# Seven-product output projections of 12 of 22 hidden chunks, inside the chain of the input projections

## The reference, cut to what matters

```python
def swiglu(x, w_in, w_out):
    gate, up = jnp.split(x @ w_in, 2, axis=-1)
    return (jax.nn.silu(gate) * up) @ w_out
# x = x + 1/2 * swiglu(rms_norm(x)); D_MODEL = 1024, D_FF = 2816
```

## Time and profile before

| | us |
|---|---|
| median of 3 runs | 2073.2 (2071.76 to 2074.09) |
| profiled execution | 2073.98 |
| span of its trace | 2071.8 |
| TensorE busy | 2041.6 (99%) |
| VectorE busy | 1329.3 (64%) |
| GpSimd busy | 1297.1 (63%) |
| ScalarE busy | 867.2 (42%) |

### The profile page before, as it was taken

The page is one execution under the profiler, slowest core; times in us unless marked ns, Lnnn a source line. Parts: engine busy times, 40 slices in busy tenths (PEclk is TensorE's granted clock), DMA queues, the critical chain, the costliest instruction groups (busy, mean ns, idle before and its releaser), DMA issues.

```text
span 2071.8 us, 41329 instructions
## 1 busy us (share of the span) xinstructions
PE 2041.6 (99%) x16420; PEld 1994.5 (96%) x16420; DVE 1329.3 (64%) x1873; ACT 867.2 (42%) x1651; POOL 1297.1 (63%) x999
## 2 busy tenths in 40 slices
PE   9999999999999999999999999999999999999998
PEld 8999999999989999999999999999998799999997
DVE  7861884425756882497578439844876678816853
ACT  6641662121574661364256226511432446505631
POOL 6775777654425676677767757765643267766773
PEclk9999999999999999999999999999999999999999
DMA  4321333122112232223123322333210232322231
GB/s 158 102 105 69 103 110 122 65 103 71 68 43 92 82 111 92 76 101 125 69 82 103 112 66 99 117 112 112 88 62 31 90 102 82 118 77 101 93 123 45
DMA packets 31702, 190.61 MB, mean 92 GB/s; under 512 B 3888, under 2 KB 6448, under 8 KB 13104
## 3 DMA queue, kind: packets, MB, share of 16 engines
q1 hardware_dynamic: 24192, 173.43, 24.3%
q10 hardware_dynamic: 7344, 14.89, 2.0%
HBM read 180.81 MB, written 7.50 MB: 91 GB/s over the span
## 4 chain that ended last, share of the span: by engine, by line
PE 52%; DVE 20%; POOL 10%; ACT 8%; issue 6%; DMA 2%; ACTq 0%; DVEq 0%; POOLq 0%; SPq 0%
PE ps L615 36%; PE ps L630 8%; DVE tg L2362 5%; POOL sil L526 4%; DVE tg L2359 4%; POOL ws L507 3%; DMA wraw<-in_wf_in 2%; POOL wl L573 2%; DVE a L2271 2%; DVE s L2300 2%; ACT sil L1761 2%; DVE ps L2280 2%; ACT ps L1692 1%; ACT ws L1725 1%; DVE ps L2338 1%
## 5 line engine op out<-in xcount | busy, mean ns | idle before, releaser
L690 PE MATMUL ps<-tt,ws 128*128 128x272 f32 x3840 | 526.2, 290 | 7.2 <-DVE ws L2304 6.4
L690 PEld LDWEIGHTS ps<-tt,ws 128*128 128x128 f32 x3840 | 500.0, 189 | 10.7 <-DVE ws L2304 7.3
L615 PE MATMUL ps<-a,wh 128*128 128x272 f32 x3028 | 500.3, 287 | 1.6 <-POOL wl L573 1.6
L573 POOL TENSOR_TENSOR wl<-wraw,wh 128x512 fp32r<-128x512 f32 (+1 forms) x351 | 475.2, 1376 | 12.7
L569 POOL TENSOR_SCALAR wh<-wraw 128x1024 fp32r<-128x1024 f32 (+2 forms) x152 | 167.7, 1103 | 471.2 <-PE ps L615 244.7
L615 PEld LDWEIGHTS ps<-a,wh 128*128 128x128 f32 x3028 | 423.6, 188 | 3.7 <-POOL wl L573 3.4
L690 PE MATMUL ps<-u,ws 128*128 128x272 f32 x2880 | 401.6, 288 | 1.1 <-DVE tg L2350 0.6
L507 POOL TENSOR_TENSOR ws<-wraw,ws 128x512 fp32r<-128x512 f32 x240 | 330.9, 1391 | 99.1 <-ACT ws L1700 55.6
L690 PEld LDWEIGHTS ps<-u,ws 128*128 128x128 f32 x2880 | 376.6, 188 | 2.4 <-issue 1.6
L615 PE MATMUL ps<-a,wl 128*128 128x272 f32 x1514 | 311.9, 287 | 0.0
L507 POOL TENSOR_TENSOR ws<-s,ws 128x512 fp32r<-128x512 f32 x160 | 209.0, 1306 | 142.3 <-ACT ws L1725 142.3
(11 more groups left out here) (391 smaller groups left out, 2929.4 us busy)
## 6 DMA issues: line engine op xcount, KB each, us to landing
wraw<-in_wf_in SPq DMA_DIRECT2D x87, 1024.0 KB, 4.8
wraw<-in_wf_out SPq DMA_DIRECT2D x32, 1408.0 KB, 6.0
wraw<-in_w_ab SPq DMA_DIRECT2D x12, 1024.0 KB, 4.8
wraw<-in_w_cd SPq DMA_DIRECT2D x10, 1024.0 KB, 4.9
wraw<-in_w_abo SPq DMA_DIRECT2D x8, 512.0 KB, 3.6
wraw<-in_w_cdo SPq DMA_DIRECT2D x8, 512.0 KB, 3.6
wraw<-in_w_bv SPq DMA_DIRECT2D x2, 1024.0 KB, 4.9
out_y<-yout ACTq DMA_DIRECT2D x14, 136.0 KB, 1.9
```

What stands on the lines that cost most here:

```text
L573: piece = nc.gpsimd.tensor_tensor(wl[:, s, some], wraw[:, par_, s * K * P + some.start: s * K * P + some.stop], wh[:, s, some].bitcast(F32 ...
L615: last = nc.tensor.matmul(bank(b0 + 2 * s + half, 0, HT), w[:, s, k * P:(k + 1) * P], act_t[:, k0 + k, part, half * HT:(half + 1) * HT], s ...
L690: last = nc.tensor.matmul(bank(b, 0, HT), ws[weights][w][:, i * P:(i + 1) * P], moving[:, part], start=(start and i == 0 and w == 0 and pa ...
```

## The change

The 22 hidden chunks are now three groups of 6, 6 and 10. The output projections of the first two groups take seven products too. They are 4 periods each of K = 6, of kind "out", put into the same chain, which now runs without a break: input periods of chunks 2 to 6, four output periods of chunks 0 to 5, input periods of chunks 7 to 12, four output periods of chunks 6 to 11, and input periods of chunks 13 to 21. The last group stays plain with K = 10.

An output period needs sums of the activation blocks of each pair of chunks (2k, 2k+1). When the odd chunk's `glu` is done, GpSimd makes four sums of 272 columns (`h_sums`), ScalarE their high parts (`e_highs`, `t3_high`), VectorE their low parts (`h_lows`, `t3_low`). This happens in one iteration of the chain per pair, six per block f; below it is called a *sum iteration*. Only half of an even chunk is still split by `glu_high` and `glu_low`. The result of an output period is added into x by VectorE (`first_row`, `second_row`). Layout of the tiles and numbering of semaphores follow. Blank lines are dropped from the diff:

```diff
-G = 2
-GK = FC // G
+GROUPS = [6, 6, 10]
-SEVENS = FC - LEAD
+SEVENS = 20 + 8
...
+        a = place("a", [11, 2, T], F32R, a_at)
+        th_at = a_at + 7 * 8 * T
+        th = place("th", [3, 3, 2, HT], F32R, th_at)
+        at[0] = th_at + 72 * HT
-        te = [place(f"te{e}", [2, HT], F32, a_at + 8 * T * 9 + 8 * HT * e) for e in range(TILES7)]
+        te = [place(f"te{e}", [2, HT], F32, th_at + 8 * HT * e) for e in range(TILES7)]
...
         SEQ = []
         for f in range(4):
-            chains = []
-            for g in range(G):
-                first = STAGE[FFN_STAGE[f] + 2 * g][1] - g * GK
-                lo, hi = max(g * GK, LEAD), (g + 1) * GK
-                chains.append([Period(first + i, SEVENS * f + i - LEAD, i, DC, (hi - 1 - i) % 2, i == hi - 1)
-                             for i in range(lo, hi)])
-            SEQ.append(chains)
+            first = STAGE[FFN_STAGE[f]][1] + LEAD
+            todo = ([("in", 0, i) for i in range(LEAD, 7)] + [("out", 0, i) for i in range(4)] +
+                    [("in", 1, i) for i in range(7, 13)] + [("out", 1, i) for i in range(4)] +
+                    [("in", 2, i) for i in range(13, FC)])
+            SEQ.append([Period(first + j, SEVENS * f + j, kind, i, DC if kind == "in" else GROUPS[g], g,
+                               (SEVENS - 1 - j) % 2, j == SEVENS - 1) for j, (kind, g, i) in enumerate(todo)])
...
+        def chunk_before(last):
+            return last.i if last and last.kind == "in" else None if last else LEAD - 1
+        def ripe(last):
+            i = chunk_before(last)
+            return i // 2 if i is not None and i < 12 and i % 2 else None
         def quarter(p, part):
...
+            def h_sums(f, k):
+                t = unit(f, TILES7 + k)
+                pool.wait_ge(glu_done, FC * f + 2 * k + 2)
+                h11, h12, h21, h22 = tg[:, 1, 0:HT], tg[:, 1, HT:T], tg[:, 2, 0:HT], tg[:, 2, HT:T]
+                e = he[slot(2 * k + 2)]
+                nc.gpsimd.tensor_tensor(e[:, T3, :], h22, h12, ALU.subtract).then_inc(t_sum, 1)
+                nc.gpsimd.tensor_tensor(e[:, 1, :], h11, h12, ALU.subtract).then_inc(t_sum, 1)
+                pool.wait_ge(t_sum, 4 * t + 1)
+                nc.gpsimd.tensor_tensor(e[:, 0, :], e[:, T3, :], h11, ALU.add).then_inc(t_sum, 1)
+                pool.wait_ge(t_sum, 4 * t + 3)
+                nc.gpsimd.tensor_tensor(e[:, 2, :], e[:, 0, :], h21, ALU.subtract).then_inc(t_sum, 1)
...
+                low_t(f, 3)
+                due = None
                 for n, p in enumerate(seq):
-                    period(seq[n - 1] if n else None, p, seq[n + 1] if n + 1 < len(seq) else None)
+                    if due is not None:
+                        h_sums(f, due)
+                    last = seq[n - 1] if n else None
+                    period(last, p, seq[n + 1] if n + 1 < len(seq) else None)
+                    due = ripe(last)
             for n, (arr, count, K) in enumerate(stages):
                 first, c0, c1, _, _ = STAGE[n]
...
+                    product(0, c0 + i, K, act_t, ready, base, slots=slots)
+                    product(1, c1 + i, K, act_t, ready, base, slots=slots)
                     if body:
                         body(i - lo)
-            def sevens(f, g):
-                seq = SEQ[f][g]
-                def operand(what, i):
+            def sevens(f):
+                seq = SEQ[f]
+                def operand(p, what, i):
+                    if p.kind == "in":
...
+                    if p.kind == "in":
+                        return tt[:, i, what]
+                    if what == T3:
+                        return rows[:, lo, :, HT:T]
+                    return th[:, i, {E2: 0, E1: 1, T4: 2}[what]]
                 def made(p, what, i):
...
-                nc.scalar.copy(a[:, slot(i), 0, :], tg[:, 1 + i % 2, :]).then_inc(act_high, 1)
-            def seven_acts(f, g, before, between):
-                seq = SEQ[f][g]
+                if i >= 2 and i % 2 == 0 and i <= 12:
+                    act.wait_ge(e_low, unit(f, TILES7 + i // 2 - 1) + 1)
+                    act.wait_ge(t3_ready, unit(f, TILES7 + i // 2 - 1) + 1)
+                cols_ = slice(0, HT if i < 12 and i % 2 == 0 else T)
+                nc.scalar.copy(a[:, slot(i), 0, cols_], tg[:, 1 + i % 2, cols_]).then_inc(act_high, 1)
+            def e_highs(f, k):
+                e = he[slot(2 * k + 2)]
+                act.wait_ge(t_sum, 4 * unit(f, TILES7 + k) + 4)
+                nc.scalar.activation(th[:, k % 3, 0, 0, :], e[:, 0, :], ACT.Identity, scale=-1.0)
+                nc.scalar.copy(th[:, k % 3, 1:3, 0, :], e[:, 1:3, :]).then_inc(e_high, 1)
+            def t3_high(f, k):
+                nc.scalar.copy(a[:, slot(2 * k), 0, HT:T], he[slot(2 * k + 2)][:, T3, :]).then_inc(t_high, 1)
...
                         high_a11(next_, p)
                     high_a22(p)
-                    if last:
+                    if last and last.kind == "in":
                         gate(last)
+                    if due is not None:
+                        e_highs(f, due)
                     snapshot2(p)
                     high_s4(p)
+                    if due is not None:
+                        t3_high(f, due)
                     if next_:
                         high_s1(next_, p)
                         high_a12(next_, p)
@@ -1796,8 +1862,9 @@
                         act.wait_ge(seven_done, sevenths(p, "P5"))
                         nc.scalar.copy(wh[:, 0, 0:GK * P], wraw[:, (p.c + 1) % 2, 0:GK * P]).then_inc(w_high, 1)
                     snapshot7(p)
-                    if last or before:
-                        glu_high(f, p.i - 1)
+                    if chunk_before(last) is not None:
+                        glu_high(f, chunk_before(last))
+                    due = ripe(last)
                 end = seq[-1]
...
+            def h_lows(f, k):
+                e = he[slot(2 * k + 2)]
+                dve.wait_ge(e_high, unit(f, TILES7 + k) + 1)
+                V.scalar_tensor_tensor(th[:, k % 3, 0, 1, :], e[:, 0, :], -1.0, th[:, k % 3, 0, 0, :].bitcast(F32),
+                                       ALU.mult, ALU.subtract)
+                V.tensor_tensor(th[:, k % 3, 1:3, 1, :], e[:, 1:3, :], th[:, k % 3, 1:3, 0, :].bitcast(F32),
+                                ALU.subtract).then_inc(e_low, 1)
+            def t3_low(f, k):
+                at_ = slot(2 * k)
+                dve.wait_ge(t_high, unit(f, TILES7 + k) + 1)
+                V.tensor_tensor(a[:, at_, 1, HT:T], he[slot(2 * k + 2)][:, T3, :], a[:, at_, 0, HT:T].bitcast(F32),
+                                ALU.subtract).then_inc(t3_ready, 1)
             def sum1(p):
                 dve.wait_ge(raw_loaded[p.c % 2], 16 * (p.c // 2 + 1))
...
+                def second_row(p):
+                    dve.wait_ge(prod_done[0], p.c + 1)
+                    dve.wait_ge(evac[0], p.c)
+                    dve.wait_ge(c_ready, 3 * p.q + 1)
+                    m = 2 * p.i + 1
+                    V.scalar_tensor_tensor(x[:, m, h2], snap7[:], 0.5, x[:, m, h2], ALU.mult, ALU.add).then_inc(snap_free, 1)
+                    V.scalar_tensor_tensor(x[:, m, h1], bank(X_BANK[p.b], 0, HT), 0.5, x[:, m, h1], ALU.mult,
+                                           ALU.add).then_inc(evac[0], 1)
                 def glu(p, then=None):
...
@@ -2369,20 +2472,27 @@
                         low1(p)
                         low2(p)
                         c11(last)
-                        if n > 1 or g == 0:
-                            glu_low(f, last.i - 1)
+                        if left is not None:
+                            glu_low(f, left)
                     if next_:
                         sum1(next_)
                     if last:
+                        if last.kind == "out":
+                            second_row(last)
                         c12(last)
                         first_row(last)
                     if next_:
                         sum2(next_)
                         sum3(next_)
-                    if last:
+                    if due is not None:
+                        h_lows(f, due)
+                    if last and last.kind == "in":
                         glu(last, p if p.end else None)
                     if next_:
                         sum4(next_)
+                    if due is not None:
+                        t3_low(f, due)
+                    due, left = ripe(last), chunk_before(last)
```

192 lines of the change are left out of this document (106 added, 86 removed).

## The result

| | before | after |
|---|---|---|
| median, us | 2073.3 (2071.76 to 2074.09, 4 runs) | 2142.5 (2140.58 to 2145.28, 4 runs) |
| ratio | | 1.0336, 95% interval 1.0318 to 1.0354 |
| span of the profiled execution, us | 2071.8 | 2143.5 |
| mean granted TensorE clock | 0.995 | 0.983 |

The change makes the kernel 3.4% slower, 69 us. The forecast was 2117 us, range 2076 to 2150: direction and range held, and the time lies 25 us above the forecast.

A forecast was written before the change was run, and what follows sets the result against it. TensorE, 99% busy, was taken as level in the chain with the loop VectorE - ScalarE - GpSimd - VectorE. 2073.98 - 36.9 (matmuls) + 35.2 (sum iterations) + 45.6 (group starts) = 2117.9, so 2117 us, range 2076 to 2150.

The forecast's parts named there:

- Gain, 36.9 us: TensorE, whole kernel: 288 matmuls fewer save 35.9 us, one chain end per block 2.8, slower chain rate costs 1.8.
- the floor: Whole kernel: 2036.4 us, the time before less the forecast gain of 36.9 us.
- Output period, 7.91 us: Output periods in the chain: 63 matmuls set 7.91 us; VectorE's 6.7 us and GpSimd's 5.5 fit in.
- Rival 3: Output periods: weight loads set the pace at 8.9 us, 32 us more, 2149; chance 0.16 together with the upper bounds.
- A sum iteration, 2.2 us each: Chain iterations with sums, 16 counted: sil 1.7 us late and `c22` 2.2 late, 35.2 us in all (0 to 4.0 each).
- time zero: In a sum iteration: the end of the last half of the preceding `glu`, from which sil's end was counted.
- Rival 1: Only group starts cost; sum iterations lose 0.4 us each, GpSimd's idle time taking the rest: 2088 us, chance 0.21.
- rival 2: VectorE and GpSimd miss each other; a group start costs 3.1 us, a sum iteration nothing: 2061 us, faster, chance 0.13.
- The first output period of a group, 5.7 us each: Group starts, 8 in all: waits of 4.2 and 1.5 us for the last sums, 45.6 us in all (3.1 to 7.5 each).
- the wait of 4.2: TensorE at a group start's fifth product: `h_lows` done at 5.0 us, 0.75 us of matmuls available, so 4.2 us standing.
- the prediction's own rule for such instructions: VectorE with two SBUF inputs: waits for GpSimd's running instruction to end, then 0.3 to 0.6 us; GpSimd loses 0.2.
- The wait of 1.5 at the seventh product: Group start: the last activation sum, behind GpSimd's sil and `glu`, comes at 9.9 us, needed at 8.4.

The follow-up runs named there:

- thin_every: Changed kernel with all activation sums of all six pairs 16 columns wide and output products waiting for none, result wrong: 2059.5 us, 0.9933 of before.
- thin_all: Changed kernel with the sums of each group's first two pairs 16 columns wide on GpSimd, ScalarE and VectorE, result wrong: 2103.3 us, 1.0146 of before.
- experiment 1: The run stale_operand: changed kernel whose output products read the second pair's sums for the third's, without waiting, result wrong: 2110.2 us.
- early_t3: early_sums with the fourth sum's parts (`t3_high`, `t3_low`) formed right behind the other sums' parts, result correct: 2093.5 us, 1.0103 of before.
- stale_operand: Changed kernel whose output products read the second pair's sums instead of the third's and don't wait for the third's, result wrong: 2110.2 us, 1.0184 of before.
- fill_wait: Changed kernel with 36 extra 128-column matmuls inside TensorE's wait for `h_lows` at each group start, result wrong: 2133.4 us, 1.0289 of before.
- early_sums: Changed kernel with the sums' high parts made before the weights' and the gate, low parts right behind `first_row`, result correct: 2118.0 us, 1.0219 of before.

## Why the prediction was right, and where its size was wrong

- **Gain, 36.9 us.** Not measured alone, but it fits within 1 us: thin_every is 14 us faster than before and 23 us above the floor, and TensorE's intervals put 22.5 of these 23 into its group starts.
- **Output period, 7.91 us.** Right: 7.9 to 8.0 for the third and fourth of every group, 8.2 to 8.7 for the second. Rival 3 (weights) is out.
- **A sum iteration, 2.2 us each, 35.2 in all.** Right in place and size: 2.0 each and 31.7 in all by TensorE's intervals, 2.45 and 39.2 by thin_all with what they pass on. The average hides a spread of 1.2 to 2.6 that was not forecast. In the iteration drawn sil ends 10.8 us after time zero (forecast 10.2). Of the parts `h_sums` took 0.76 to 0.79 with one in contention at 1.09 on average (forecast 0.75), and the waits were 1.15 for the snapshot (forecast 1.1) and 0.5 for `c22` (forecast 0.9). Rival 1 and rival 2 fall with this.
- **The first output period of a group, 5.7 us each, 45.6 in all. This is the step that failed, as a term that was too small:** it is 8.5 each by VectorE's intervals, 68 in all, and 9.2 each by TensorE's, 74.0 in all. That is 28 us more than forecast; the sum iterations took 3.5 less, and the difference is the 25 us missed. Three things were off. First, the wait of 4.2 was 5.16. The text lists for `h_lows` "0.5 of waiting on average and 0.3, and another wait and 0.6", but its sum goes from 3.6 to 5.0, which is 0.5, 0.3 and 0.6: the other wait was counted as nothing. The two took 1.13 and 1.85, 2.98 for 1.4 (1.01 and 1.85 on average over all 24). The first ended 0.29 us after GpSimd's low parts did (103.00), the second 0.59 after the multiplication of sil (104.48), so the prediction's own rule for such instructions held, and each met GpSimd's running instruction. They started 0.65 us sooner than forecast, which took off some of it. Second, the clock was not in the sum at all: 1.5 us per group start. Third, my account ended with the second wait, but the period is late in VectorE's loop too: with the first wait taken away (experiment 1) 4.2 us per group start stayed, and with the sums away as well still about 2.
- **The wait of 1.5 at the seventh product.** It came at five of eight group starts, 1.2 us at four of them, but through another path: not `glu` and GpSimd's sil, which were done long before (VectorE idles 4.47 us ahead of `sum4`), but the loop over `snapshot2` and S4's low part, which starts only once the first wait is over. Early_t3 shows it: with `t3_low` off that loop the wait is gone.

The excess of 106 us above 2036.4 splits along the runs, in this order: 39 us with the sums of the first two pairs (thin_all), 32 the group start waits for the last pair's sums (stale_operand), 11.5 these last sums otherwise (2142.5 - 39.2 - 32.3 = 2071.0, thin_every 2059.5), 23 the rest of a group start and small waits. That the first two simply add is my assumption, and the third is only what is left between them and thin_every, so it is as uncertain. TensorE's intervals need no such assumption: 31.7 in the sum iterations and 74.0 in the group starts, of which stale_operand leaves 40.0 and thin_every 22.5.

The Trainium skill (SBUF — State Buffer, Who interferes with whom), cited in the prediction, is borne out: 128x544 with both inputs in SBUF takes 1.85 us beside GpSimd and 0.71 in its pause, and 32 columns take 1.38 on average. I had the rule and still priced the average case.

No version tried that computes the reference beats the kernel before. The best of them, early_t3, is 1.0% slower. By TensorE's intervals the sum iterations still cost it 24.8 us, 1.55 each, and the group starts 32.5 us, 4.1 each; the two take more than the gain of 36.9. Whether the fourth sum and half of the low parts could be put into the iteration after, where both engines have some room, was not tried.

## What to carry to other kernels

When a loop over three engines is level with TensorE, matmuls saved by adding activation sums are paid for in that loop: price each added instruction at its contended time, and put it beside the idle us of its engine in that iteration, not of the whole span. Where TensorE has to stand, add the clock, and follow the loops that restart only when the wait ends, since they form the next wait. In this kernel VectorE instructions with two SBUF inputs did best where GpSimd waited for something else: at the one group start of early_t3 where that pause of 0.3 us was missing, TensorE's wait was 1.3 us longer.

## What the runs showed of the hardware that was not expected

The granted clock fell to its lower level, 0.50, in the middle of the kernel around waits of TensorE of 1.2 to 5.2 us, and the matmuls behind them ran at half rate for 3.4 us (early_t3) to 5.6 us (after). That costs 1.2 to 1.5 us on top of the wait. In after it falls during the wait; around the shorter waits it falls between 0.3 us before TensorE starts again (fill_wait) and 1.3 us after (early_t3). In the group start of early_sums shown above the wait ended at 102.13 and 0.80 was granted in 102 to 103. It isn't regular: after waits of 5.2 us it fell 8 times of 8, after waits of 2.9 us 6 of 8 (early_sums), after 1.73 us 4 of 7, and at the eighth of the same run, 3.04 us long, it stayed up (early_t3). Around waits of 1.24 us it fell 5 of 8 times (fill_wait), and around waits of 1.4 to 1.9 us twice in 8 (thin_every). The rows of TensorE there and of the windows:

```profile
1134.29 1.77 PE L737 MATMUL ps<-th,ws 128*128 128x272 f32 x12 [3.04 <-DVE th L2345]
```
```profile
1131.00:1134.00 3.00, 0.26 (x3) 0.04 (x1) 2.97 (x5) 1.29 (x3) 3.00 (x4) 1.00 0.00 0
1134.00:1136.00 2.00, 1.71 (x13) 1.71 (x14) 2.00 (x3) 0.00 (x0) 1.45 (x1) 1.00 0.49 169
```

What decides between these cases stays open.
